# A wait taken early, a result stored one unit sooner, and splits put ahead of convolutions in a two-layer streaming encoder kernel

## The reference

```
h = x * (1 + sc_m) + sh_m
a_qkv, a_z, a_a, a_b, b_q, b_k, b_v = split_cols(h @ w_in, EVEN_WIDTHS)
a_qkv = silu(causal_conv(a_qkv, conv_w))             # q, k, v of the DeltaNet
...
for e in range(N_EXPERTS):
    out = out + combine[:, e:e + 1] * swiglu(t, w_up[e], w_down[e])
```

## Time and profile before

| what | value |
|---|---|
| median of three runs | 1743.6 us |
| the profiled execution, its device time | 1742.85 us |
| its span, first to last instruction | 1740.9 us |
| TensorE matmul busy | 1617.3 us (93%) |
| VectorE busy | 1282.3 us (74%) |
| ScalarE busy | 1009.3 us (58%) |
| mean granted TensorE clock | 0.966 |
| DMA over the span | 299 GB/s |

### The profile page before, as it was taken

The page is one execution under the profiler, slowest core; times in us unless marked ns, Lnnn a source line. Parts: engine busy times, 40 slices in busy tenths (PEclk is TensorE's granted clock), DMA queues, the critical chain, the costliest instruction groups (busy, mean ns, idle before and its releaser), DMA issues.

```text
span 1740.9 us, 20082 instructions
## 1 busy us (share of the span) xinstructions
PE 1617.3 (93%) x7810; PEld 1297.4 (75%) x7810; DVE 1282.3 (74%) x1160; ACT 1009.3 (58%) x867; POOL 132.8 (8%) x94
## 2 busy tenths in 40 slices
PE   4888996999969999879999999999999999999996
PEld 1874765787858777658888888888888888888875
DVE  1374536655456665688889888898898898988986
ACT  1432223444434444347777777777777777777775
POOL 0421310000000100220000000000000000000005
PEclk8898998999989999979999999999999999999998
DMA  9347885855454543539999999999999999999993
GB/s 329 130 167 283 322 316 193 285 183 185 169 169 146 164 171 145 187 129 391 388 379 390 375 388 387 369 388 379 376 389 375 381 388 371 384 385 367 385 382 151
DMA packets 234370, 515.33 MB, mean 296 GB/s; under 512 B 8936, under 2 KB 40960, under 8 KB 234176
## 3 DMA queue, kind: packets, MB, share of 16 engines
q1 hardware_dynamic: 228272, 491.99, 77.3%
q10 hardware_dynamic: 2992, 11.79, 1.9%
q0 software_dynamic: 3008, 10.20, 1.9%
HBM read 507.15 MB, written 13.11 MB: 299 GB/s over the span
## 4 chain that ended last, share of the span: by engine, by line
PE 86%; DVE 7%; issue 2%; ACT 2%; DMA 2%; POOL 1%; DVEq 0%; SPq 0%; ACTq 0%; POOLq 0%
PE bank L762 25%; PE bank L764 25%; PE bank L763 25%; PE bank L741 2%; PE bank L925 2%; DMA ring<-in_cond_w 2%; PE bank L1185 1%; PE bank L757 1%; DVE arena L1768 1%; DVE small L1689 1%; PE bank L774 0%; ACT w_part L1310 0%; DVE w_part L1643 0%; DVE hs L1715 0%; PE bank L1167 0%
## 5 line engine op out<-in xcount | busy, mean ns | idle before, releaser
L1654 DVE TENSOR_TENSOR w_lo<-ring,w_hi 128x2048 fp32r<-128x2048 f32 x336 | 764.7, 2290 | 104.1 <-ACT w_hi L1537 102.2
L1537 ACT ACTIVATE w_hi<-ring 128x2048 fp32r<-128x2048 f32 x334 | 640.5, 1918 | 196.3 <-PE bank L764 187.0
L762 PE MATMUL bank<-w_lo,heT_hi 128*128 128x512 f32 x896 | 353.8, 395 | 3.8 <-DVE w_lo L1654 2.2
L764 PE MATMUL bank<-w_hi,heT_hi 128*128 128x512 f32 x896 | 349.7, 390 | 0.0
L763 PE MATMUL bank<-w_hi,heT_lo 128*128 128x512 f32 x896 | 348.9, 389 | 0.0
L1643 DVE TENSOR_TENSOR w_part<-ring,w_part 128x1024 fp32r<-128x1024 f32 x148 | 183.4, 1246 | 211.0 <-ACT w_part L1310 206.2
L1310 ACT ACTIVATE w_part<-ring 128x1024 fp32r<-128x1024 f32 (+1 forms) x162 | 169.1, 1049 | 252.0 <-PE bank L764 247.3
L762 PEld LDWEIGHTS bank<-w_lo,heT_hi 128*128 128x128 f32 x896 | 168.3, 188 | 39.0 <-issue 5.9
L764 PEld LDWEIGHTS bank<-w_hi,heT_hi 128*128 128x128 f32 x896 | 168.2, 188 | 35.9
L763 PEld LDWEIGHTS bank<-w_hi,heT_lo 128*128 128x128 f32 x896 | 168.5, 188 | 33.6
L762 PE MATMUL bank<-w_part,hT_hi 128*128 128x512 f32 (+1 forms) x448 | 179.8, 401 | 14.2 <-DVE w_part L1643 13.1
(11 more groups left out here) (344 smaller groups left out, 1586.8 us busy)
## 6 DMA issues: line engine op xcount, KB each, us to landing
ring<-in_moe_w_up SPq DMA_DIRECT2D x224, 1024.0 KB, 8.8
ring<-in_moe_w_down SPq DMA_DIRECT2D x112, 1024.0 KB, 7.8
ring<-in_cond_w SPq DMA_DIRECT2D x24, 2048.0 KB, 9.1
ring<-in_ffn_w_up SPq DMA_DIRECT2D x22, 1024.0 KB, 8.2
ring<-in_od_w_in SPq DMA_DIRECT2D x8, 2048.0 KB, 7.9
ring<-in_ev_w_in SPq DMA_DIRECT2D x5, 2048.0 KB, 12.4
ring<-in_ffn_w_down SPq DMA_DIRECT2D x5, 2048.0 KB, 7.7
ring<-in_od_w_in SPq DMA_DIRECT2D x8, 1024.0 KB, 8.0
```

Of the source, the lines that this page charges most:

```text
L762: mm(bank, lhs[0], rhs[1], start=start, stop=False)
L764: return mm(bank, lhs[0], rhs[0], start=False, stop=stop)
L1537: f(w_hi[:, n % 3], half_landed(act, it, u, half), ACT.Copy) \
L1654: tt(w_lo[:, buf], at, w_hi[:, buf].bitcast(F32), ALU.subtract).then_inc(S["w_lo"], 1)
```

## The change

Three things are changed.

1. TensorE, units 0 to 2 of `ev_in`: the four banks of a unit are asked for at the start of the unit, all four before its first matmul. Before, each bank was asked for where its first matmul comes (and again, without effect, for the parts that follow).
2. Experts: VectorE's `gated` stands at the head of unit 4 in place of unit 5, ScalarE's `result` at the head of unit 5 in place of unit 6. This is so in seven of the eight items; the first item has no earlier one.
3. VectorE in `ev_in`: each group of splits stands one place earlier in relation to the three convolutions.

```
             for u in range(3):
+                outs = [to_fill(pe, "ev_in", u, i) for i in range(4)]
                 for j in range(4):
                     w = part("ev_in", u, j)
-                    for i in range(4):
-                        bank, full = to_fill(pe, "ev_in", u, i)
+                    for i, (bank, full) in enumerate(outs):
...
-                    if u == RESULT_UNIT + 2 and earlier is not None:
+                    if u == RESULT_UNIT + 1 and earlier is not None:
                         result(earlier)
...
+            split_ahead("ev_in", 1)

             taken(dve, "convT")
             for i in range(3):
-                split_ahead(*(("ev_in", 1), ("ev_in", 2), ("ev_in", 5))[i])
+                split_ahead(*(("ev_in", 2), ("ev_in", 5), ("ev_in", 4))[i])
...
-            split_ahead("ev_in", 4)
             split_ahead("ev_in", 3)
...
-                    if u == RESULT_UNIT + 1 and earlier is not None:
+                    if u == RESULT_UNIT and earlier is not None:
                         gated(earlier)
```

## The result

The changed kernel takes 1752.58 us (median of six runs, 1751.16 to 1755.71), the kernel before 1743.3 us (six runs, 1740.38 to 1744.97). The medians differ by 9.3 us; the ratio is 1.0056, with a 95% interval of 1.0046 to 1.0066, which is 8.0 to 11.5 us slower. The prediction was 1753.2 us.

What follows compares the result with a forecast made beforehand. The prediction took TensorE, busy 93% of the span, as the bound. Banks 3.4, splits 0 and experts 6.6 us sum to +10.0 us, forecast 1753.2 us; its own range was 1751 to 1755.5, the wider one 1747 to 1757.

Steps and rivals of the forecast that it cites:

- The banks: Input projection, units 1 and 2: each first matmul waits 1.6 us for the fourth bank; with restarts 3.4 us, bounds 0 to 4.4.
- The splits: Input projection: the wait saved before unit 5 is waited out again before unit 4; gain 0, bounds -3 to +3 us.
- part 14 ties the first convolution to the end of unit 2: VectorE, input projection: split 14 needs unit 2 ended, so the first convolution starts at 93.26, in the second's former slot.
- the longer wait would not lengthen the slow stretch: Unit 4, input projection: a 6.2 us wait costs the same 2.8 us slow-clock stretch as 4.94 us, not up to twice.
- The gate arithmetic: VectorE behind the third convolution: takes 8 us, ends near 137, stays hidden by about 5 us.
- GpSimd's 3.8 us in the prediction: Convolution beside two GpSimd instructions totalling 3.8 us: loses 2.95 us by the trace, the full 3.8 by the skill's rule.
- The experts: Unit 4 in seven items: `gated` makes the product late for the transposes, 0.94 us each, 6.6 us; bounds 0 to 9.0.
- The sum: Whole kernel: bank, split and expert terms, 3.4 + 0 + 6.6, make it 10.0 us slower.
- those that leave one term out: Only one side costs: bank waits absorbed, 1750.2 us (7%), or the experts' product wait absorbed, 1747.0 us (5%).
- The clock did not fall in the experts: Rival: each 0.94 us gap in the experts brings a slow stretch, 19.6 us on top, 1772.8 us; chance 2%.
- The faster one: Rival: TensorE was held by VectorE's queue in unit 5 of each item; up to 9.0 us saved, 1738.0 us; chance 4%.

Runs made afterwards that it cites:

- the kernel with three: Kernel before, with three of a unit's four banks asked for at its start, the fourth at its first matmul: 1742.96 us, ratio 1.0001.
- that of part 2: Kernel before, with only `gated` moved to the head of unit 4 and `result` to unit 5 in the experts: 1750.15 us, ratio 1.0037.
- that of part 3: Kernel before, with only VectorE's groups of splits in `ev_in` one place earlier relative to the convolutions: 1742.82 us, ratio 1.0002.
- part 1 alone: Kernel before, with only the four banks asked for at the start of each of units 0 to 2 of `ev_in`: 1745.47 us, ratio 1.0018.
- splits in another grouping: Kernel before, with VectorE's splits 12, 14, 16, 18 in a row after the first convolution, 20 and 22 after the second: 1739.66 us, ratio 0.9981.
- half in front: Kernel before, with only the first of `gated`'s two instructions moved ahead of unit 4's product, `result` left in place: 1745.48 us, ratio 1.0015.
- all of it behind the product: Kernel before, with `gated` in unit 4 but behind its product, and `result` in unit 5: 1744.2 us, ratio 1.0011.
- the DMA without effect: Kernel before, with `gated` moved ahead of unit 4's product and `result` with its DMA left in unit 6: 1749.28 us, ratio 1.0036.

## Why the prediction was right

**The banks.** Forecast 3.4 us. In the trace the two waits and their restarts move unit 4 by 108.43 - 103.92 - 0.8 = 3.7 us; alone, part 1 costs 1.0018 x 1742.8, 3.1 us (1.6 to 4.7). The mechanism and the bank (the fourth, by the kernel with three) are shown. The small excess is the time from the start of the copy to the matmul, 0.62 us where I had put the duration of a copy plus 0.06, 0.45 us. Unit 4 was to start near 107.3; without the 0.8 us of this trace's start it did at 107.6.

**The splits.** Forecast 0; measured 0.3 us (-1.2 to +1.9). The step on which it rested, that part 14 ties the first convolution to the end of unit 2, holds: the wait before unit 4 became 6.27 us (6.2 forecast), with the same 9.24 us of convolution in front. That the longer wait would not lengthen the slow stretch was a choice between two values, and the forecast had some luck in it: behind waits of 4.94 or 6.27 us the clock stayed low for 5.9 to 6.2 us of unit 4 in seven traces, the changed kernel's among them, for 3.3 us in that of part 2 and for 2.9 us in that of part 3. The length of the wait does not tell these apart. In one point the working was luckier than it knew: with part 1 in, the wait before unit 5 goes anyway, so part 3 had nothing of its own left to win there. The gate arithmetic took less time than I had put behind the third convolution (132.95 to 138.84, 5.9 us, not 8), and stayed hidden with 8.5 us to spare and not 5. The working had missed that 2.2 of the 8 us were one small instruction of line 1786 that ran beside a GpSimd instruction (2.35 us, the six like it 0.17 us each); GpSimd's instruction now falls into the third convolution.

On why the convolution takes 9.2 us the traces say more than the prediction did. The third one, now beside one GpSimd instruction of 2.64 us, takes 8.3 us from 124.61 on in place of 6.25, and all of it is in one of its 16 instructions (GpSimd's, the VectorE instruction that started behind it, and one that ran undisturbed):

```profile
128.41 2.64 POOL L2228 TENSOR_TENSOR w_part<-ring,w_part 128x1024 fp32r<-128x1024 f32 x1 [5.21 <-ACT w_part L1310]
128.69 2.64 DVE L1769 SCALAR_TENSOR_TENSOR arena<-arena,small 128x256 f32<-128x256 f32 x1
132.16 0.48 DVE L1769 SCALAR_TENSOR_TENSOR arena<-arena,small 128x256 f32<-128x256 f32 x1
```

An instruction of the convolution's multiply-and-add line (1769, or 1768) that starts while a GpSimd instruction runs ends 0.28 to 0.29 us behind it, here and everywhere else in the input projection of the eleven traces. The whole convolution follows: 6.26 us beside no GpSimd work but for the last 0.4 us, 8.4 us beside one instruction of 2.4 to 2.7 us (8.45 with part 1 alone), 9.3 us beside one of 1.3 and one of 2.36 us, 10.6 us beside two of 2.4 us (splits in another grouping). The Trainium skill (SBUF — State Buffer, section "SBUF: two separate sides") has whichever of the two starts second blocked until the other is done. The trace agrees: the 2.64 us of line 1769 end 0.28 us behind GpSimd's 2.64. The loss was smaller than GpSimd's 3.8 us in the prediction since VectorE's instruction already under way goes on, and since of its own 0.48 us the held one needs only 0.28 behind the end of the stop.

**The experts.** Forecast 7 x 0.94 = 6.6 us; measured in the windows 7 x 0.9 = 6.3, and alone 1.0037, 6.4 us (4.0 to 8.9). The dose shows the mechanism: half in front 0.3 us an item, all in front 0.9 us, all of it behind the product next to nothing, and the DMA without effect.

**The sum.** 3.4 + 0 + 6.6 = 10.0; the three parts alone give 3.1 + 0.3 + 6.4 = 9.8 us, the change 9.3. They add, since each delays TensorE at a place where it is the bound. The sum is right for its terms and not by terms that cancel. Of the rivals, those that leave one term out are excluded by the runs of each part. The clock did not fall in the experts: it is 1.00 in the windows. The faster one had named VectorE's queue in unit 5; moving `gated` out of it, behind the product, gave no item less than 118.6 us.

## What to carry to other kernels

An engine that sets the pace pays for each wait that is asked too early: take a wait just ahead of the instruction that needs it, and count when the resource comes free, not how many waits the program has. For a small job on a helper engine, the place matters more than its length: look for the margin between the helper's result and its use, and put the job behind the result that is needed next. And where a group of splits stands behind a long side job, the split that the pacing engine waits for (here part 16, then part 20) has to get in front of the job; moving others gains nothing. Then look again, for the next late one.

## What the runs showed of the hardware

That the same idle time of TensorE is followed by a slow stretch in one execution and not in the next was not expected. Behind 2.1 us of idle time near 666 us the granted clock fell in five of the eleven traces here and not in six; behind 2.32 us near 1691 us it fell in four and not in seven. The matmuls of 512 columns came 0.43 us apart or 0.23 us, and the row of eight transposes took 1.94 or 1.07 us. A slow stretch spared at 666 us was in part paid later: in those six traces the low clock near 738 us lasted 17.1 us, where it lasted 13.7 in four of the other five, and against the kernel before 0.9 to 1.1 us of the 1.5 us went again. The gaps of 0.7 to 1.6 us that this change made left the pace alone in every trace, and behind those of 4.94 and 6.27 us it was slow in all nine traces that have one.

That two engines hold each other up can be seen in single instructions. A multiply-and-add of VectorE that takes 0.48 us alone takes up to 2.66 us beside a GpSimd instruction of 2.4 to 2.6 us, so the same convolution takes 6.3 to 10.6 us by what falls beside it.
